# Two-layer hybrid decoder step on one core: the first four projection tiles made together, row by row, with the norm product a tile later

## The reference

```python
def project_layer(x, pos, norm_g, w_in):
    h = rms_norm(x, norm_g)              # x * norm_g / sqrt(mean(x**2) + 1e-6)
    pr = split(h @ w_in)                 # keys, queries, values, gates of three mixers
    k = rope(k, pos); q = rope(q, pos)   # rotation by position
    ...
for l in range(DEPTH):
    xp, new_p = layer_prompt(xp, weights[l])
    xs, new_s = layer_sample(xs, caches[l], weights[l])
y = rms_norm(x, final_norm_g)
```

## Time and profile before

| | |
|---|---|
| median of three runs | 915.12 us (914.53 to 917.81) |
| profiled execution | 913.02 us, of which the span from first to last instruction is 911.4 us |
| TensorE busy | 894.7 us, 98% of the span |
| VectorE busy | 647.6 us, 71% |
| ScalarE busy | 454.4 us, 50% |
| GpSimd busy | 194.3 us, 21% |
| DMA | 209.96 MB, 230 GB/s on the mean |
| mean granted clock of TensorE | 0.998 |

### The profile page before, as it was taken

The page is one execution under the profiler, slowest core; times in us unless marked ns, Lnnn a source line. Parts: engine busy times, 40 slices in busy tenths (PEclk is TensorE's granted clock), DMA queues, the critical chain, the costliest instruction groups (busy, mean ns, idle before and its releaser), DMA issues.

```text
span 911.4 us, 21368 instructions
## 1 busy us (share of the span) xinstructions
PE 894.7 (98%) x7904; PEld 837.2 (92%) x7904; DVE 647.6 (71%) x1449; ACT 454.4 (50%) x900; POOL 194.3 (21%) x321
## 2 busy tenths in 40 slices
PE   7999999999999999999999999999999999999997
PEld 6999998888888799999999999898888978999996
DVE  6999776677667467656769996676766565775664
ACT  6444665465443544334553447664654444443352
POOL 1200000348658300000000000013574771000000
PEclk9999999999999999999999999999999999999999
DMA  9762995736979873333675587866569899345321
GB/s 331 300 227 97 427 355 207 303 142 183 315 236 289 268 326 147 139 140 125 257 255 193 204 320 265 305 269 246 189 181 301 248 273 347 149 155 206 149 94 52
DMA packets 66359, 209.96 MB, mean 230 GB/s; under 512 B 12192, under 2 KB 49776, under 8 KB 56272
## 3 DMA queue, kind: packets, MB, share of 16 engines
q1 hardware_dynamic: 57200, 187.67, 56.2%
q0 software_dynamic: 8912, 20.92, 7.1%
q10 hardware_dynamic: 144, 0.01, 0.0%
HBM read 202.58 MB, written 41.36 MB: 268 GB/s over the span
## 4 chain that ended last, share of the span: by engine, by line
PE 89%; SPq 4%; DMA 3%; issue 2%; ACT 1%; DVE 1%; DVEq 0%; ACTq 0%
PE bank L1056 65%; PE bank L1316 8%; PE bank L1069 4%; SPq L880 4%; DMA paged<-in_pool 2%; PE bank L1194 2%; PE bank L1186 1%; PE bank L1350 1%; PE bank L1223 1%; PE bank L1447 1%; PE bank L1236 1%; PE bank L1249 1%; DMA x<-in_x 1%; PE bank L1418 1%; PE bank L1295 0%
## 5 line engine op out<-in xcount | busy, mean ns | idle before, releaser
L1828 DVE TENSOR_TENSOR big_r<-big,paged_r 128x1024 fp32r<-128x1024 f32 (+1 forms) x160 | 194.6, 1221 | 72.5 <-ACT paged_r L1582 71.5
L1056 PE MATMUL bank<-xnT_high_r,paged_r 128*128 128x288 f32 x768 | 231.4, 301 | 0.0
L1056 PE MATMUL bank<-xnT_r,paged_r 128*128 128x288 f32 x704 | 207.7, 295 | 0.0
L1056 PE MATMUL bank<-xnT_high_r,big_r 128*128 128x288 f32 x704 | 207.2, 294 | 0.0
L1582 ACT ACTIVATE paged_r<-big 128x1024 fp32r<-128x1024 f32 (+1 forms) x160 | 166.7, 1049 | 4.8 <-DMA big<-in_w_feat 2.7
L1056 PE MATMUL bank<-short_r,big_r 128*128 128x288 f32 x568 | 167.5, 295 | 0.0
L1056 PEld LDWEIGHTS bank<-xnT_high_r,paged_r 128*128 128x128 f32 x768 | 144.0, 188 | 4.0 <-issue 2.0
L1056 PEld LDWEIGHTS bank<-xnT_high_r,big_r 128*128 128x128 f32 x704 | 132.5, 188 | 0.0
L1056 PEld LDWEIGHTS bank<-xnT_r,paged_r 128*128 128x128 f32 x704 | 132.3, 188 | 0.0
L1056 PE MATMUL bank<-short_r,paged_r 128*128 128x288 f32 x440 | 130.9, 298 | 1.1 <-DVE big_r L1828 0.9
L1056 PE MATMUL bank<-kvp_r,paged_r 128*128 128x288 f32 x440 | 130.4, 296 | 0.0
(11 more groups left out here) (353 smaller groups left out, 1804.7 us busy)
## 6 DMA issues: line engine op xcount, KB each, us to landing
big<-in_w_tok SPq DMA_DIRECT2D x13, 2048.0 KB, 9.0
big<-in_w_feat SPq DMA_DIRECT2D x12, 2048.0 KB, 8.5
big<-in_w_gate SPq DMA_DIRECT2D x10, 2048.0 KB, 8.6
out_kept_dil<-in_cache_dil SPq DMA_DIRECT2D x16, 1020.0 KB, 13.3
paged<-in_pool SPq DMA_DIRECT2D x218, 64.0 KB, 4.2
big<-in_w_up SPq DMA_DIRECT2D x12, 1024.0 KB, 8.7
paged<-in_pool POOLq DMA_DIRECT2D x166, 64.0 KB, 4.6
big<-in_kv_win SPq DMA_DIRECT2D x4, 2048.0 KB, 8.9
```

What stands on the lines that cost most here:

```text
L1056: last = mm(out, l, r, start=(c == 0 and i == 0), stop=(c == n - 1 and i == 2))
L1828: v.tensor_tensor(l_part[:, rest], full[:, rest], h_part[:, rest].bitcast(FP32), ALU.subtract)\
```

## The change

The first four tiles of layer 0 are made together. For each row c: 4 products of high weights with high x, 4 with low x, 4 of low weights with high x, into four banks (the two of `PJ`, and the two of `SC` for tiles 2 and 3). The weights of the first block come from a new input `w_first`, which has them row by row (512 columns a row), in six pieces on SP's queue, and rounding and splitting go row by row as well (steps `first`). The squares of x stand among the rows. The second block comes in four pieces with a semaphore each, the first of them issued ahead of the constants; the small tensors of the layer are issued behind the third block, where they stood behind the second. The norm product (`root`, `rots`) stands behind tile 4 and tile 8's weights, where it stood behind tile 3 and tile 7's weights. TensorE begins with nine products of 128x128 ones with 128 columns of ones into bank 7, whose result nobody reads, as soon as the ones are set. The order at the start of layer 0 is now:

```diff
     for i in range(len(TILES)):
+        if (layer, i) == (0, 0):
+            out += tile_splits(4) + [("square", 6), ("square", 7)] + tile_splits(5)
         out.append(("proj", i))
-        if i == 0:
-            out += [of_tile("split", 2), of_tile("round", 3)]
-            if layer == 0:
-                out += [("square", 3), of_tile("split", 3)] + [("square", z) for z in range(4, KT)]
-            else:
-                out += [of_tile("split", 3), ("root",), ("rots",)]
-        elif i < 4:
-            out += tile_splits(*({1: (4,), 2: (5, 6), 3: (7,)}, {1: (4, 5), 2: (6,), 3: (7,)})[layer][i])
-        else:
+        if i == 0 and layer:
+            out += [of_tile("split", 2), of_tile("round", 3), of_tile("split", 3), ("root",), ("rots",)]
+        elif 0 < i < 4:
+            out += tile_splits(*({2: (6,), 3: (7,)}, {1: (4, 5), 2: (6,), 3: (7,)})[layer].get(i, ()))
+        elif i:
             last_low = [("nlow", KT - 1)] if NORM_AT.get(i - 2) == KT - 1 else []
             out += last_low + tile_splits(*[n for n in (i + 4,) if n < len(TILES) + SPLIT_AHEAD])
-        if (layer, i) == (0, 3):
+        if (layer, i) == (0, 4):
             out += [("root",), ("rots",)]
...
-    starts = [start(0, i) for i in range(KT)]
-    out = sum(starts[0:2], []) + [(0, ("firsthalf",))] + sum(starts[2:4], []) + halves(0, 0) + sum(starts[4:], []) + [(0, ("square", 0))] + halves(0, 1)
-    out += [(0, ("square", 1)), (0, ("square", 2)), (0, ("round", ("tok", 0), 2))]
+    out = []
+    for c in range(KT):
+        out += start(0, c) + [(0, ("square", z)) for z in {2: (0, 1)}.get(c, ())] + [(0, ("first", c))]
+        out += [(0, ("square", c - 2))] * (c >= 4)
...
+    FIRST_ROWS = ((0, 1), (1, 2), (2, 3), (3, 4), (4, 6), (6, 8))
...
             load_x(0)
-            load_first_half(0, first_of_all_in)
+            load_first(0)
+            load_first(1)
             load_x(1)
-            load_first_half(1, first_in[0])
             sp.wait_ge(x_in[0], 16)
-            load_x(2)
-            load_x(3)
-            load_first(1)
-            sp.wait_ge(x_in[2], 16)
             load_first(2)
             load_first(3)
+            load_x(2)
+            sp.wait_ge(x_in[1], 16)
+            load_first(4)
+            load_x(3)
+            load_first(5)
+            load_second(0)
             for dst, src in CONSTS:
                 sp.dma_start(dst, src).then_inc(const_in, 16)
...
-                    if key == ("tok", 1 if layer == 0 else 0):
+                    if (layer, key) == (0, ("tok", 1)):
+                        for q in range(1, 4):
+                            load_second(q)
+                        continue
+                    if key == ("tok", 2 if layer == 0 else 0):
                         layer_loads = [(w_gc[:, :, :], a["w_gc"][layer]), (conv_w[:, :, :], a["conv_w"][layer]),
...
         def _(pool):
-            pool.wait_ge(*BIG.is_full(("tok", 1), 0))
+            pool.wait_ge(second_in[3], 16)
...
+            pe.wait_ge(ones_ready, 1)
+            for _ in range(WARM_UP):
+                mm(ps[7][:, 0:P], ones[:, :], ones[:, :], start=True, stop=True)
...
+                elif k == "first":
+                    c = s[1]
+                    four = [("proj", q) for q in range(4)]
+                    pe.wait_ge(*first_rounded.at(s))
+                    pe.wait_ge(*x_split.at(("start", c)))
+                    for z in (xg_high, xg_low):
+                        for q in range(4):
+                            mm(proj_bank(four[q])[:, 0:T], first_high[:, c, q, :], z[:, c, :], start=(c == 0 and z is xg_high),
+                               stop=False)
+                    pe.wait_ge(*first_split.at(s))
+                    for q in range(4):
+                        last = mm(proj_bank(four[q])[:, 0:T], first_low[:, c, q, :], xg_high[:, c, :], start=False,
+                                  stop=(c == KT - 1))
+                        if c == KT - 1:
+                            last.then_inc(*proj_ring(0, four[q]).fill(four[q]))
```

More of the change, by code:

```diff
@@ L559, in trunk_program @@
     in_turn_bank = lambda s: s[0] == "kc" or s == ("impsum", 0)
+    in_score_bank = lambda layer, s: layer == 0 and s in (("proj", 2), ("proj", 3))
     for layer, s in ALL:
         k = s[0]
-        if k in ("proj", "gc", "feat", "gkc", "kc", "vc", "gate", "up", "down", "imp", "impsum") and not in_turn_bank(s):
+        if in_score_bank(layer, s):
+            sc_keys.append((layer, s))
+        elif k in ("proj", "gc", "feat", "gkc", "kc", "vc", "gate", "up", "down", "imp", "impsum") and not in_turn_bank(s):
             pj_keys.append((layer, s))
@@ L611, in trunk_program @@
         big_keys += [("kA", hb), ("win", hb), ("vA", hb)]
-    BIG = Ring(nc, "big", layered(big_keys), 3, by=16, free=False, first=2, given=[(0, ("tok", 0))], restart=True)
+    BIG = Ring(nc, "big", layered(big_keys), 3, by=16, free=False, first=2, given=[(0, ("tok", 0)), (0, ("tok", 1))], restart=True)
     gate_keys = [("gate", fh, i) for fh in range(2) for i in range(3)] + [("down", nh) for nh in range(2)]
@@ L762, in trunk_program @@
     x_in = [nc.alloc_semaphore(f"x{i}_in") for i in range(KT // 2)]
-    first_of_all_in, first_rounded, first_split = (nc.alloc_semaphore("first_half_" + z) for z in ("in", "rounded", "split"))
-    first_in = [nc.alloc_semaphore(f"first_weights{q}_in") for q in range(4)]
+    first_rounded, first_split = (Signal(nc, "first_rows_" + z, all_of("first")) for z in ("rounded", "split"))
+    FIRST_ROWS = ((0, 1), (1, 2), (2, 3), (3, 4), (4, 6), (6, 8))
+    first_in = [nc.alloc_semaphore(f"first_rows{i}_in") for i in range(len(FIRST_ROWS))]
+    second_in = [nc.alloc_semaphore(f"second_weights{q}_in") for q in range(4)]
+    by_row = lambda z: z.rearrange("p (c q n) -> p c q n", c=KT, q=4)
+    first_raw, first_high, first_low = by_row(bigb(("tok", 0))), by_row(high(("tok", 0))), by_row(low(("tok", 0)))
     g_in, const_in, late_in = [nc.alloc_semaphore(n) for n in ("norm_g_in", "constants_in", "late_constants_in")]
@@ L814, in big_used @@
         if kind == "tok":
-            return PJ.is_full(("proj", 4 * key[1] + 3), layer)
+            last = ("proj", 4 * key[1] + 3)
+            return proj_ring(layer, last).is_full(last, layer)
         if kind == "feat":
@@ L1111, in _ @@
                     wh, wl = parts_of(("tok", g), q4)
[L1112 to L1124, removed]
                     precise(pj(s)[:, 0:T], lambda c: (wh[:, c, :], wl[:, c, :]),
@@ L1534, in _ @@
                         continue
-                    f(dst, pj(s)[:, 0:T], ACT.Copy, scale=SCALE if kind == "q" else 1.0).then_inc(*PJ.release(s))
+                    f(dst, proj_bank(s)[:, 0:T], ACT.Copy, scale=SCALE if kind == "q" else 1.0)\
+                        .then_inc(*proj_ring(layer, s).release(s))
                 elif k == "vturn":
@@ L1561, in _ @@
                     item, q = s[1:]
-                    if (layer, item) == (0, ("tok", 0)):
-                        act.wait_ge(first_in[q], 16)
+                    if (layer, item) == (0, ("tok", 1)):
+                        act.wait_ge(second_in[q], 16)
                     elif item == FIRST:
@@ L1580, in _ @@
                         act.wait_ge(*PJ.is_full(("gate", 0, 0, 3)))
-                    rest = slice(512, 1024) if (layer, item, q) == (0, ("tok", 0), 0) else slice(0, None)
-                    f(high_part(item, q)[:, rest], split_part(bigb(item), item, q)[:, rest], ACT.Copy)\
+                    f(high_part(item, q), split_part(bigb(item), item, q), ACT.Copy)\
                         .then_inc(*high_done.inc(s))
[L1584 to L1588, removed]
+                elif k == "first":
+                    c = s[1]
+                    act.wait_ge(first_in[[first <= c < end for first, end in FIRST_ROWS].index(True)], 16)
+                    f(first_high[:, c, :, :], first_raw[:, c, :, :], ACT.Copy).then_inc(*first_rounded.inc(s))
                 elif k == "gc":
@@ L1826, in _ @@
                     dve.wait_ge(*high_done.at(("round", item, q)))
-                    rest = slice(512, 1024) if (layer, item, q) == (0, ("tok", 0), 0) else slice(0, None)
-                    v.tensor_tensor(l_part[:, rest], full[:, rest], h_part[:, rest].bitcast(FP32), ALU.subtract)\
+                    v.tensor_tensor(l_part, full, h_part.bitcast(FP32), ALU.subtract)\
                         .then_inc(*split_done.inc(s))
-                elif k == "firsthalf":
-                    item = ("tok", 0)
-                    h_part, l_part, full = (split_part(z, item, 0)[:, 0:512] for z in (high(item), low(item), bigb(item)))
-                    dve.wait_ge(first_rounded, 1)
-                    v.tensor_tensor(l_part, full, h_part.bitcast(FP32), ALU.subtract).then_inc(first_split, 1)
+                elif k == "first":
+                    c = s[1]
+                    dve.wait_ge(*first_rounded.at(s))
```

(2 more changed lines are left out.)

33 lines of the change are left out of this document (19 added, 14 removed).

## The result

| | before | changed |
|---|---|---|
| median of 22 runs each | 915.43 us (914.27 to 917.91) | 918.29 us (915.38 to 922.05) |
| changed over before | | 1.0031 [1.0022, 1.004] |
| profiled execution / span | 913.02 / 911.4 us | 922.05 / 919.1 us |

The change makes the kernel 2.9 us slower. That is above the forecast range (917.0), though within the 0.5% that I called "same".

A forecast was written before the change was run, and what follows sets the result against it. TensorE (PE) was taken as the bound, the question being tile 8's start: landing 24.3 + chain 12.4 = 36.7, 0.25 us sooner than 36.95. Span 911.1, profiled execution 912.7, median 914.8 us; range 912.4 to 917.0.

The forecast's parts named there:

- The four tiles: Start of layer 0: PE at full rate from 5.83, four tiles done at 18.6 instead of 22.20, 3.6 us less.
- Where the gain goes: Norm product behind tile 8's rounding: root, reciprocal and rotations queue behind one DMA; PE waits about 2.6 us before the transposes.
- chain of 12.37 us: ACT and DVE steps from the third weight block's landing (L) to tile 8's start (T8), summed to 12.37 us.
- The landing of tok 2: Third block of weights (tiles 8 to 11) lands, time L, at 24.3 us instead of 25.6; bounds 22.5 and 25.6.
- 0.8 for the small tensors: DMA queue: small layer tensors (250 KB) issued behind the third block save 0.6 us plus some 0.2 for short pieces.
- 0.5 for the lull: DMA queue at 9 to 10 us: the wait for an earlier x piece fills part of the lull, 200 KB, 0.5 us.
- rival B: Third block lands no sooner, sharing engines with late constants; at 25.6 tile 8 starts at 38.0, 916.2 us; chance 0.12.
- The clock (C): PE's clock falls in the new wait; some 14 products of tile 6 step 0.24, 1.5 us, total 916.2; chance 0.07.
- The total: Whole kernel: span 911.1, median 914.8 us where it was 915.12; same within 0.5% given 0.93.
- D: Start: warm-up does nothing, four tiles end at 20.1, hidden by the new wait; 914.8 us; forecast with it 0.50.
- A: Gain arrives in part: third block lands at 22.5 to 23.5, tile 8 1.0 to 2.1 us sooner; chance 0.24.
- Behind tile 8: Rest of the kernel: nothing of the change remains; the end moves by as much as tile 8's start.

The follow-up runs named there:

- after_d: The changed kernel with no edit, a fourth trace; span 918.2 us.
- after_c: The changed kernel with no edit, another trace; span 917.2 us.
- before_root_late: The kernel before with only the root and rotation factors moved behind the weights of tile 8; ratio 1.002 to before.
- no_ones: The changed kernel without the nine products of ones at the start; ratio 1.0036 to before.
- after_again: The changed kernel once more, no edit, for a second trace; ratio 1.0024 to before.
- three_in_one: The changed kernel with the last three quarters of the second block loaded as one transfer; ratio 1.0041 to before.
- second_whole: The changed kernel with the second block in one transfer behind the constants, instead of four pieces; ratio 1.0061 to before.
- ones_in_wait: The changed kernel with fourteen more products of ones ahead of PE's wait for the reciprocal; ratio 1.0033 to before.
- root_ahead: The changed kernel with the root and rotation factors ahead of the weights of tile 8, still behind tile 4; ratio 0.9984 to before.

## Why the prediction was right or wrong

**The four tiles.** Right in kind, off by 2.3 us. PE began at 5.37. It was not at full rate from the first product, as I had taken it: the first eight cost 0.8 us more (0.9 in after_d, next to nothing in after_c). Then it waited 1.6 us for row 4: its piece of 512 KB landed at 13.5, 6.7 us after its issue. I had written that pieces arrive fast enough, at 400 GB/s; at 8 to 10 us the rate was 184. Tile 4 began at 21.27, not 18.95; the four tiles ended 1.5 us sooner than before, not 3.6. This cost nothing, as the later wait covers it.

**Where the gain goes.** Right: root, reciprocal and rotations queue behind a rounding that waits for all of tok 2. The chain of 12.37 us was measured at 12.4 in before_root_late.

**The landing of tok 2.** This is the step that failed. I took 24.3 us as a fall from 25.6, by 0.8 for the small tensors and 0.5 for the lull. Measured were 28.3, 27.5, 26.7 and 27.5. The saving at the lull was wrong: the wait on SP's queue that I read as filling it makes it deeper (184 GB/s at 8 to 10 us; second block in at 21.6 to 21.9 us in the four traces, where the old queue has 19.6 to 20.4; L 1.0 us later on the mean instead of 0.5 sooner). The saving of 0.8 for the small tensors did not show. Also, 25.6 was the earliest of four landings of the old queue (mean 26.2), and I took it as a constant. For rival B I held nothing in the rows to be able to delay tok 2 by 3.6 us; here it was 2.7 in the worst trace. B's reason did not occur: I had the late constants a microsecond sooner, but they wait for the second block, and their first issue is at 21.9 to 22.2 us in the four traces of the changed kernel, at 19.9 to 20.7 in the three of before.

**The clock (C).** The forecast put this term at nothing and gave it 0.07; it happened in all traces of the changed kernel. The price was right: T8 - L is 13.5 to 13.7 in most, 1.1 above 12.4 (14.4 in after_d, where 19 products were slow). The wait came out at 3.2 to 4.2 us rather than 2.6, but the fall also came with 2.5 us in no_ones, so the landing isn't what decided it. The sum with both corrections, 28.3 + 12.4 + 1.1 = 41.8, meets the 42.03 of the trace.
The Trainium skill, TensorE: Matmul & The Clock Gate, section "HAM oscillation — how this bites in real kernels", says that a wait for a DMA between groups of products puts PE back to half clock. I discounted it; here the trace agrees, with a granted clock of 0.50 and 0.24 us per product behind a wait that ends on a DMA.

**The total.** With C and a mean L of 27.5, tile 8 is at 41.0 (41.3 in the four traces), 3.6 us behind the 37.4 of three traces of before. The medians differ by 2.9, of which some 0.7 are outside the span, where the start of tile 8 explains nothing; the traces show slower executions than the median. B and C were priced one by one. Together, with L at 25.6, they give 39.1 and 917.3 us by my own numbers, above my range, and I never added them. D did not occur as I put it: the ones did shorten the slow start, from 14 products to eight or fewer. That the time would be the same without them was right, by no_ones. A did not occur: the earliest landing in any trace is 25.1.

**Behind tile 8.** I forecast that nothing of the change remains there. The rest of 7.7 - 5.1 us in the first two profiles is no more than the difference in PE's waits for the page loads, 5.6 us in this trace and 2.3 in the first of before, where other traces of before have up to 4.3. On the mean span less T8 is 1.6 us longer in the changed kernel. In after_again and after_d the granted clock also falls to 0.50 near 300 us, in no trace of before. Whether that comes from the change or is chance, these few traces don't tell.

## What to carry to other kernels

When a stretch is made shorter, look for what the next stretch hangs on: if an engine's ordered list puts a step for the present behind one that waits for a transfer for later, the gain stops there, and moving one line in the order is worth more than the new start. Treat a landing time from one trace as a sample; within one kernel it strayed by as much as the shift that I forecast (1.3 us). And a wait on the issuing queue has to be priced by the bytes that it keeps from being moved, summed over the whole stretch, not by the one slow window in which it shows.

## What was unexpected of the hardware

- With a wait of PE of 2.5 to 5.2 us and then 1.3 us of one-column transposes, PE went to 1.2 GHz for 12 to 14 products of 288 columns, in after_d for 19; after a wait of 1.3 us (three_in_one) for 24. It did so too after a wait of 0.84 us (second_whole), 1.1 us behind the first product, and after one of 0.64 us behind 3.3 us of ones (ones_in_wait), 1.6 us behind it. With no wait (root_ahead) or 0.90 us (before_root_late) ahead of the same transposes it did not, nor after 2.1 us ahead of tile 4 in three_in_one, with full products behind. What tells these cases apart is open.
- The 18 records of nine full-precision products of 128 columns took 4.21 us at the start of the kernel (3.7 to 4.2 in all traces that have them), 0.47 each (I had estimated 0.44), and 28 records took 3.29 us in the wait, 0.235 each: twice as fast, as at full clock.
- A transfer is as late as its slowest share. In the profile of the changed kernel 15 of the 16 increments of tok 2's semaphore were there at 25.5 us, and the last at 28.3; in the first profile of before both came at 25.6. In the three other traces of the changed kernel the last share came 0.5 to 0.9 us behind the one before it. Why one share lags is open.
